# Two background programs change places between the two gather stages of a two-block transformer kernel

## What is computed

```python
def chunk(xc):                                   # 128 tokens at a time
    q = (xc @ wq).reshape(PEER_CHUNK, PEER_HEADS, 2, half)
    sc = jnp.einsum('chpd,hpnd->chpn', q, sub_keys)
    s1, i1 = lax.top_k(sc[:, :, 0], 16); s2, i2 = lax.top_k(sc[:, :, 1], 16)
    ...                                          # top 16 of the 256 pair sums: eidx, 8 heads x 16
    u_sel = jnp.take(u, eidx, axis=0)
    a = gelu(einsum('chkd,cd->chk', u_sel, xc))
    v_sel = jnp.take(v, eidx, axis=0)
    return einsum('chk,chkd->cd', softmax(top_s) * a, v_sel)
```

```python
sh1, sc1, g1, sh2, sc2, g2 = silu(c) @ w_mod + b_mod     # six vectors of 1024: "modulation"
cm = silu(c_ctx) @ w_mod[:, :2 * D] + b_mod[:2 * D]      # two more, from the same weights
hc = rmsnorm(ctx) * (1 + cm[1]) + cm[0]                  # 256 context tokens
sf_c = _state_features(hc, w_in, gdn_conv)                # four projections, gates, two convolutions
init = _recurrent_mixers(sf_c)                           # retention and gated-delta states, 2 directions x 2 chunks
```

## Time and profile before

| | |
|---|---|
| Time, median of 3 runs (lowest, highest) | 3003.76 us (3003.11, 3008.64) |
| Time of the profiled execution, and its span | 3003.76 us, 3001.9 us |
| Busy share of PE, DVE, ACT, POOL | 81%, 53%, 28%, 28% |
| Mean granted TensorE clock | 0.925 |
| Gather stage of layer 0, first to last `dots` | 233.5 to 935.8 us |
| Gather stage of layer 1, first to last `dots` | 1155.0 to 1890.2 us |

### The profile page before, as it was taken

The page is one execution under the profiler, slowest core; times in us unless marked ns, Lnnn a source line. Parts: engine busy times, 40 slices in busy tenths (PEclk is TensorE's granted clock), DMA queues, the critical chain, the costliest instruction groups (busy, mean ns, idle before and its releaser), DMA issues.

```text
span 3001.9 us, 29482 instructions
## 1 busy us (share of the span) xinstructions
PE 2422.6 (81%) x9692; PEld 1323.7 (44%) x9692; DVE 1599.1 (53%) x3289; ACT 836.0 (28%) x2272; POOL 835.0 (28%) x723
## 2 busy tenths in 40 slices
PE   7898888888887888998887899779797786676664
PEld 3684322333333766454444455558783532222221
DVE  4556657485444636758889877356544521121111
ACT  1313333333332412343443444223210111111110
POOL 1004333343331102334544546011020112122221
PEclk9899999999999899999999999989998788888887
DMA  6029999999998126999898999512113299999994
GB/s 275 1 85 391 422 422 422 422 408 422 422 400 347 57 85 258 375 375 395 357 421 314 359 421 396 207 43 71 43 57 130 116 410 396 390 391 380 383 383 157
DMA packets 129842, 885.93 MB, mean 295 GB/s; under 512 B 23184, under 2 KB 23568, under 8 KB 31760
## 3 DMA queue, kind: packets, MB, share of 16 engines
q0 software_dynamic: 86976, 553.74, 45.9%
q1 hardware_dynamic: 42704, 330.22, 27.4%
HBM read 877.56 MB, written 37.75 MB: 305 GB/s over the span
## 4 chain that ended last, share of the span: by engine, by line
PE 43%; DMA 25%; DVE 22%; ACT 4%; issue 3%; SPq 1%; POOL 1%; DVEq 0%; ACTq 0%; POOLq 0%
PE ps L155 41%; DMA ring<-in_peer_uv,idx_u 13%; DMA ring<-in_w_gu 7%; DVE ring L1307 6%; DVE arena L76 6%; ACT arena L125 3%; DMA ring<-in_w_down 3%; PE ps L158 2%; DMA arena<-in_w_gu 1%; DVE arena L109 1%; SPq L2560 1%; DVE arena L1307 1%; DVE arena L97 1%; DVE iu L113 1%; DVE ring L76 1%
## 5 line engine op out<-in xcount | busy, mean ns | idle before, releaser
L155 PE MATMUL ps<-ring,arena 128*128 128x512 f32 (+3 forms) x3264 | 1254.8, 646 | 282.2 <-ACT arena L125 162.9
L155 PEld LDWEIGHTS ps<-ring,arena 128*128 128x128 f32 (+2 forms) x3264 | 470.1, 179 | 950.5 <-issue 591.0
L1307 DVE CUSTOM_DVE_ANT_0 ring<-ring,h 128x1024 f32<-128x1024 f32 x448 | 563.2, 1257 | 332.7 <-DMA ring<-in_peer_uv,idx_u 299.5
L2377 POOL DMA_INDIRECT ring<-in_peer_uv,idx_u x448 | 496.5, 1108 | 751.7 <-PE ps L155 613.5
L155 PE MATMUL ps<-arena 128*128 128x128 f32 (+7 forms) x2504 | 497.5, 381 | 120.5 <-ACT arena L125 51.6
L125 ACT ACTIVATE arena<-arena 128x1 f32<-128x1 f32 (+4 forms) x1097 | 296.7, 270 | 750.4 <-DVE arena L1307 650.1
L155 PEld LDWEIGHTS ps<-arena 128*128 128x128 f32 (+3 forms) x2504 | 312.7, 193 | 278.6 <-issue 152.9
L76 DVE TENSOR_TENSOR arena<-arena,ps 128x512 f32<-128x512 f32 (+1 forms) x158 | 93.7, 593 | 448.0 <-ACT arena L125 363.9
L125 ACT ACTIVATE arena<-ps 128x512 f32<-128x512 f32 (+4 forms) x198 | 109.8, 554 | 793.8 <-PE ps L155 718.7
L155 PE MATMUL ps<-ring,hT 128*128 128x512 f32 (+2 forms) x896 | 309.8, 506 | 19.5 <-DVE hT L97 11.9
L125 ACT ACTIVATE arena<-cst,arena 128x128 f32<-128x128 f32 x512 | 205.5, 401 | 157.5 <-PE ps L155 117.2
(11 more groups left out here) (117 smaller groups left out, 1487.6 us busy)
## 6 DMA issues: line engine op xcount, KB each, us to landing
ring<-in_w_gu SPq DMA_DIRECT2D x98, 1024.0 KB, 29.0
ring<-in_w_down SPq DMA_DIRECT2D x52, 1024.0 KB, 30.4
ring<-in_w_in SPq DMA_DIRECT2D x16, 2048.0 KB, 12.5
arena<-in_w_gu SPq DMA_DIRECT2D x30, 1024.0 KB, 30.7
ring<-in_w_mod SPq DMA_DIRECT2D x12, 2048.0 KB
ring<-in_peer_wq SPq DMA_DIRECT2D x8, 2048.0 KB, 8.0
ring<-in_w_o SPq DMA_DIRECT2D x6, 2048.0 KB, 11.0
ring<-in_w_gates SPq DMA_DIRECT2D x12, 1024.0 KB, 4.8
```

The source lines that it names most:

```text
L155: return self.e.matmul(o, lhsT, rhs, start=start, stop=stop, skip_group_check=True)
L1307: v.done(v.e.tensor_tensor_reduce(out=row, in0=row, in1=h[:, n // 128, :], scale=1.0, scalar=0.0, op0=ALU.mult, op1=ALU.add, accum_out=aa[ ...
L2377: g.e.indirect_dma_start(out=landing(n), out_offset=None, in_=d["peer_uv"], in_offset=bass.IndirectOffsetOnAxis(ap=idx_u[:, n:n + 1], axis ...
```

## The change

It moves phases and loads; no arithmetic is added or taken away. modulation() is cut in two. Layer 0 now carries blocks 0 to 3 of w_mod (14 phases), and then the whole context chain (116 phases); layer 1 carries blocks 4 to 11 (18 phases). The steps at which phases are taken change: in layer 0 one every second step from 2 to 128 and from 138 to 252, and one more at each of 195, 203, ... 251 (130 phases); in layer 1 one every 5 steps from 4 to 89. So phase p of the context chain is taken at step 30 + 2p up to step 128 (p = 49) and at 138 + 2(p - 50) up to step 194 (p = 78), and from there five phases in every eight steps instead of four. SP's loads follow.

```diff
 def beside(l, n):
     if l:
-        return 1 if n in range(10, 130, 2) or n in range(138, 250, 2) else 0
-    return 1 if n in range(12, 246, 9) else 0
+        return 1 if n in range(4, 94, 5) else 0
+    return 1 if n in range(2, 130, 2) or n in range(138, 254, 2) or n in range(195, 254, 8) else 0
...
-            def modulation():
+            def modulation(i0, i1):
...
-                for i in range(12):
-                    if i:
+                for i in range(i0, i1):
+                    if i > i0:
                         columns(i - 1)
...
-                    yield from idle(2)
-                columns(11)
+                    yield from idle(3 if i < 4 else 2)
+                columns(i1 - 1)
...
                 attention(l)
-                if l:
-                    peer(l, chain(context_rows(),
+                if l == 0:
+                    peer(l, chain(modulation(0, 4), context_rows(),
                                   conv_features(ctx_side, hcT, ctx_side.conv_blocks, 0, OTHERS), idle(5),
                                   context_states()))
                 else:
-                    peer(l, modulation())
+                    peer(l, modulation(4, 12))
...
                 block(16, 4, d["w_o"][l, 1], ("loaded", "w_o", l, 1),
-                      after=[("used", "w_mod", 11)] if l else [("used", "ln0")])
+                      after=[("used", "ctx", "Gv")] if l else [("used", "ln0")])
...
-                if l:
-                    load(ctx_rows, rows_of(d["ctx"]), s_ctx, ("loaded", "ctx"), after=[("out", "s", 1, 1, 3)])
-                    ctx_block(0, "Rk", before)
+                if l == 0:
+                    load(ctx_rows, rows_of(d["ctx"]), s_ctx, ("loaded", "ctx"), after=[("out", "s", 0, 1, 3)])
+                    modulate(range(0, 4), before)
+                    ctx_block(0, "Rk", ("used", "w_mod", 3))
...
                 else:
-                    modulate(range(12), before)
-            block(16, 4, d["w_in2"][4], ("loaded", "x", "Rq"), after=[("used", "ctx", "Gv")])
+                    modulate(range(4, 12), before)
+            block(16, 4, d["w_in2"][4], ("loaded", "x", "Rq"), after=[("used", "w_mod", 11)])
```

More of the change, by code:

```diff
@@ L1341, in peer, with modulation @@
                 v.tell(("used", "ln2", l))
-            def modulation():
+            def modulation(i0, i1):
                 yield
                 yield
-                for i in range(12):
-                    yield
+                for i in range(i0, i1):
+                    yield from idle(2 if i < 4 else 1)
                     v.wait_ge(*at("ps", "mod columns", i))
@@ L2547, in gpsimd_program @@
                 attention(l)
-                if l:
-                    peer(l, chain(context_rows(), conv_features(ctx_side, ctx_side.conv_blocks, 0), idle(5),
+                if l == 0:
+                    peer(l, chain(idle(14), context_rows(), conv_features(ctx_side, ctx_side.conv_blocks, 0), idle(5),
                                   context_states()))
                 else:
-                    peer(l, idle(26))
+                    peer(l, idle(18))
             second()
```

## The result

| | before | changed |
|---|---|---|
| Median of the first comparison (lowest, highest) | 3004.48 us (3003.11, 3008.64) | 3027.69 us (3025.4, 3030.31) |
| Ratio to before, 95% interval | | 1.0073 (1.0061 to 1.0085) |
| Span of the profiled execution | 3001.9 us | 3023.7 us |
| Gather stage, layer 0 | 702.3 us | 770.8 us |
| Gather stage, layer 1 | 735.2 us | 686.5 us |

The change made the kernel slower by 0.73%, some 23 us. The forecast was 3004.7 us, and its range ended at 3016.

What follows compares the result with a forecast made beforehand. Layer 0 was taken as bound by transfers, layer 1 partly by them and partly by DVE and PE. Stages of 687.4 + 750.1 + 0.9 = 1438.4 us against 1437.5 gave 3004.7 us; own range 2998 to 3010, outer 2987 to 3016.

Steps and rivals of the forecast that it cites:

- The first half of the argument: Both gather stages: layer 1 falls to 687.4 us, layer 0 rises to 750.1 us if its stalls move unchanged.
- the late block: Layer 0's start: w_mod block 0 lands behind the context rows, PE waits some 5 us; costed at nothing, 5 without cover.
- the exchange cancels: Both stages: -47.8 us in layer 1 and +47.8 in layer 0 cancel to first order.
- term 0: Steps 128 to 176, routing unit 3 with the norm: DVE's sum and the time stay the same; bounds -12 and +5.
- DVE's waits for gathers: Layer 0's stage after the change: a sign that the forecast is right, some 65 us.
- the collisions were the loss: Rival, middle stretch and chunk 1 start: up to 12 us and 7.7 come back, 2987 to 2996 us; chance 0.33.
- The dense end: Steps 194 to 252, 38 phases: PE's work 5.2 us over the transfers, half taken: +2.6, bounds 0 and +8.
- the starts of chunks 3 and 4: Heavy phases at 194 to 198 and 224 to 228: +3 (bounds 0 and +6) and +1 us.
- The start of chunk 1 and the convolutions: Chunk 1 start at 110 to 116: -7.7 us (-9.8 to 0); start, rows and convolutions: +2 (-5 to +10).
- the dense end makes PE the limit: Rival, layer 0's end: PE needs over 2.48 us a step, +11, so 3015 us; chance 0.18.
- two signs: Layer 0's end: DMA under 0.95 and PE over 95% would show that the dense end is the loss.
- POOL and DVE meet more often: Rival, layer 0: POOL's 24 level operations could each shut out a `dots`; +10, so 3013 us; chance 0.10.

Runs made afterwards that it cites:

- e4: The kernel before, with all 116 context phases of layer 1 at the steps they have in the changed kernel: 3023.48 us, ratio 1.0063.
- e17: The changed kernel, with DVE's phases one step later and POOL's two gathers later: 3007.21 us, ratio 0.9998 to the kernel before.
- e6: The changed kernel, leaving out half of the context's level products on PE: one execution, 3024.17 us.
- e2: The changed kernel, with the eight extra phases moved from the end to 29 to 35 and 130 to 136: 3023.82 us, ratio 1.0063.
- e5: The kernel before, with a pause after the convolutions and the four chunks at every second step from 104 to 254: 3007.85 us, ratio 0.9994.
- e8: The kernel before, with context phases 60 to 115 of layer 1 taken six steps later: 3005.4 us, ratio 0.999.
- e10: The changed kernel, with each background phase of DVE one step later than PE's, in both layers: 3017.47 us, ratio 1.0039.
- e3: The changed kernel, with w_mod block 0 loaded ahead of the context rows in SP's queue: 3026.01 us, ratio 1.0067.
- e9: The changed kernel, with the end's eight extra phases among the levels, at 203 to 215 and 233 to 245: one execution, 3024.92 us.
- e12: The changed kernel, with the end's eight extra phases at the chunk starts, 195 to 201 and 225 to 231: one execution, 4266.46 us.
- e16: The kernel of e12 run once more, with nothing changed: one execution, 3020.52 us.

## Why the prediction was wrong

**What held.** The first half of the argument did: transfers decide the stage with modulation alone (686.5 us, 687.4 forecast), three blocks more cost the other their transfer time (17.1 us between e4 and the changed kernel, of which 2.6 are the late block, leaving 14.5; 14.9 forecast), and to first order the exchange cancels. Steps 128 to 176 took 24.5 us over for 26.4 (26.2 in e4), term 0: DVE's sum hardly changed (128.8 us, 130.2 in e4, for 133.0), and neither did the time. DVE's waits for gathers in that stage, forecast at some 65 us after the 66.5 of the earlier trace rows, were 59.9. The rival in which the collisions were the loss got nothing there: up to 12 us were to come back in these 48 steps, and 1.9 did.

**What failed: the terms of the denser steps.** The step of the prediction at fault is "The dense end", with the starts of chunks 3 and 4. It added 3 + 1 + 2.6 = 6.6 us to the 9.7 that steps 176 to 255 took before. The steps of the change in the kernel before (e4) take 29.0 there, 19.3 more where 6.6 were forecast: a miss of 12.7 us, and more than even the upper bounds together would have given (6, 1 and 8). Steps 194 to 252 of the changed kernel, for which the prediction gave 150 to 155 us, took 173.4. Three things were wrong in it.

- I took one phase for 1.2 us of PE. The level window had been divided with 1.8 us a sum; where sums follow one another they cost 1.72 (12 records of three sums in 5.43 us, of which the last record's own tail is 0.3), which leaves 58.0 - 41.3 = 16.7 for 12 phases, 1.4 each. Ten phases in 16 steps are then 41.5 us of PE for 39.7 of transfers. The stretch was 4.7 over; with both edits of order (e17) it is 2.2, near this sum, and with half of the products (e6) 0.3. The error is small, though: with the new prices the 59 steps need 154.3 us of PE instead of 151.8.
- I halved the result since the starts "carry less PE work". They do, but DVE has its most work there (24.9 of 28.6 us in steps 192 to 200, where PE has 23.5; in 200 to 216 PE has 41.1 of 44.4 and DVE 27.4), so the two engines are the fullest in turn, and neither stretch gives back what the other lost. In a sum of busy times over the end, PE has 165 and DVE 136 of 186 us, and neither looks full.
- I added engine times and left out order. DVE waits within a phase for PE with its next `dots` behind, POOL within a phase for DVE with its next gathers behind. POOL's wait for DVE stood in the earlier trace rows; DVE's for PE, 9.3 us in steps 176 to 255 of the kernel before, the prediction doesn't name; neither was priced for the dense end. e17 shows what order was worth in the changed kernel: 17 us of the stage, 9.5 of them in the end.

As a rough account of steps 194 to 252: they took 26.8 us over the 146.6 of transfers, of which PE's sum of work at the new prices is 7.7, and 11.4 went with the two edits of order (162.0 us in e17). The 7.7 that are left no run explains.

**The start of chunk 1 and the convolutions.** Forecast +2 and -7.7. In e4 steps 0 to 128 take 64.9 us over for 65.8: -0.9, a miss of 4.8. In the prediction's own terms, the steps up to the end of the convolutions take 61.0 over for 56.2 (0 to 104 in e4, 0 to 88 before), +4.8 for +2, and those with the start of chunk 1 take 3.9 for 9.6 (104 to 128 in e4, 88 to 128 before), -5.7 for -7.7; both are within their bounds. In the changed kernel steps 104 to 120 took 41.6 us, 42 forecast. Most of what the start gave back came again in front of it, with the convolutions in routing unit 2. e2, e5 and e8 show the same in this stage: phases moved off one stall made another. Which single wait makes it in the convolutions was not tried apart; e10 gives back 6 us there.

**The late block.** Costed at nothing, since gathers were queued; e3 gives 2.6 us of the 7 that PE waited.

Of the 18.9 us by which the two stages miss (1457.3 for 1438.4), 12.7 and 4.8 are these terms as e4 has them, 2.2 are what the changed kernel's stage has beyond e4 and three blocks, and the stage of layer 1 is 0.9 short; 0.1 is rounding and steps 128 to 176. Of the rivals, "the dense end makes PE the limit" was nearest, slower and in the right place. But its 3015 us counted PE alone, and of its two signs only one came: DMA is at 0.86 over the end, PE at 89% (165.0 of 186.1 us) and not over 95%. "POOL and DVE meet more often" did not happen: `dots` averages 1.27 us in the stage of the changed kernel and 1.29 in that of before, and the longest is 2862 ns for 2798. Over their median of 1226 ns the `dots` of the stage lose 11 us in all, where they lost 17. The exclusion that the Trainium skill states ("SBUF — State Buffer", "SBUF: two separate sides") fits the longest `dots` of both kernels, each over twice the median of 1226 ns.

## What to carry to other kernels

When work is interleaved by hand into a stage that a transfer bounds, sums of busy time don't give its price. Here five phases in eight steps instead of four cost 24 us in 63 steps, though the fullest engine was busy 165 of 186 us, and moving phases elsewhere (e2, e5, e8, e9) mostly moved the stall. For each in-order engine list what stands behind a wait in its queue, above all the issue of the next transfers; two such waits can cover for each other, so test them together before calling either harmless. Here a step of offset for DVE and two gathers for POOL, each worth nothing alone in the kernel before, were worth 12 us together and 17 with the phases placed off the busiest stretch.

## What the hardware did that I had not expected

One execution in e12 took 4266.46 us, and the same kernel 3020.52 in e16. These are PE's busy share and its granted clock in the slices of e12; in e16 the clock's digit is 7 or more in every slice:

```profile
PE   8999999999999999999999999999898988899996
...
PEclk9999999995555555555555555555555555555555
```

A slice is 106.6 us here. From 1000 us to the end the granted clock is 0.55 on average, so near the lower of its two levels, 1.2 GHz. PE had not paused before it fell: it was busy 329 of the 330 us from 630 to 960 us. But the clock's row is not the whole of it. The first gather stage began at 350.0 us, where in e16 it began at 232.1, though the digits are at 9 up to there. The same products of PE, first in e12 from 350 to 900 us and then in e16 from 240 to 900 us (busy us, mean ns of one, idle time before them):

```profile
L155 PE MATMUL ps<-ring,arena 128*128 128x512 f32 x360 | 340.6, 1146 | 4.6 <-ACT arena L125 4.6
L155 PE MATMUL ps<-ring,arena 128*128 128x512 f32 x826 | 396.7, 626 | 65.5 <-ACT arena L125 65.3
```

From 1000 to 1600 us of e12 the mean is 968 ns. So the products were slowest where the row reads full. The trace of e12 has no record of the clock before 956.1 us, where that of e16 begins at 22.7, so the nines there may show nothing. Either way PE is busy 4070 us of the execution, and the chain that ended last is PE's for 93%. Single executions in two other runs, of 4101.84 and 7859.29 us beside medians of 3025.74 and 3007.21, have no profile; their granted clocks are on record as 0.563 and 1.0, so the slowest of all has the full clock. The granted clock as recorded doesn't account for these times, and their cause stays open. Nothing in the kernel differs between e12 and e16.
